# Feed-forward with gate and up products two chunks ahead of the down products, and every inner value turned by DMA

## The reference

```python
def swiglu(x, w_gate, w_up, w_down):
    return (jax.nn.silu(x @ w_gate) * (x @ w_up)) @ w_down

h = h + FFN_RES * swiglu(rms_norm(h, g), w_gate, w_up, w_down)   # T = 256, D = 1024, D_FF = 2816
```

## Time and profile before

| | us |
|---|---|
| median of 3 runs | 1210.16 |
| lowest and highest of them | 1208.95, 1210.77 |
| span of the profiled execution | 1207.7 |
| TensorE busy | 1199.7 |
| VectorE busy | 773.3 |
| ScalarE busy | 691.9 |

### The profile page before, as it was taken

The page is one execution under the profiler, slowest core; times in us unless marked ns, Lnnn a source line. Parts: engine busy times, 40 slices in busy tenths (PEclk is TensorE's granted clock), DMA queues, the critical chain, the costliest instruction groups (busy, mean ns, idle before and its releaser), DMA issues.

```text
span 1207.7 us, 17122 instructions
## 1 busy us (share of the span) xinstructions
PE 1199.7 (99%) x5662; PEld 989.7 (82%) x5662; DVE 773.3 (64%) x1089; ACT 691.9 (57%) x1012; POOL 68.3 (6%) x119
## 2 busy tenths in 40 slices
PE   9999999999999999999999999999999999999998
PEld 7888888877788888888888788888888887888887
DVE  6665555688685556567678766665556667655554
ACT  6555555676655555557666576655555546655543
POOL 0420000000000000000220110000000000000000
PEclk9999999999999999999999999999999999999999
DMA  9977754554465998745654517986655554776771
GB/s 333 245 226 223 216 178 154 167 175 140 157 220 166 244 245 257 217 155 160 201 168 164 174 66 232 252 230 198 200 155 167 164 168 145 213 221 201 219 226 44
DMA packets 208385, 232.01 MB, mean 192 GB/s; under 512 B 56080, under 2 KB 148368, under 8 KB 208336
## 3 DMA queue, kind: packets, MB, share of 16 engines
q1 hardware_dynamic: 163792, 214.61, 57.1%
q10 hardware_dynamic: 42752, 11.02, 5.0%
q0 software_dynamic: 1792, 5.75, 2.0%
HBM read 219.78 MB, written 1.05 MB: 183 GB/s over the span
## 4 chain that ended last, share of the span: by engine, by line
PE 96%; DVE 1%; DMA 1%; ACT 1%; issue 0%; ACTq 0%
PE bank L1971 30%; PE bank L1973 30%; PE bank L1972 30%; PE bank L2030 2%; PE bank L2198 1%; DMA sb_probs<-sb_probs 1%; PE bank L2214 1%; PE bank L2185 1%; PE bank L2183 0%; DMA sb_gates<-h_xT 0%; ACT sb_probs L1237 0%; PE bank L2060 0%; DVE sb_wl L1320 0%; PE bank L2502 0%; DVE sb_rmax L1866 0%
## 5 line engine op out<-in xcount | busy, mean ns | idle before, releaser
L1971 PE MATMUL bank<-sb_wh,sb_aTh 128*128 128x512 f32 (+1 forms) x1124 | 435.6, 388 | 0.0
L1973 PE MATMUL bank<-sb_wh,sb_aTl 128*128 128x512 f32 (+1 forms) x1124 | 431.0, 383 | 0.0
L1972 PE MATMUL bank<-sb_wl,sb_aTh 128*128 128x512 f32 (+1 forms) x1124 | 430.7, 383 | 0.0
L1320 DVE TENSOR_TENSOR sb_wl<-sb_raw,sb_wh 128x1024 fp32r<-128x1024 f32 x269 | 325.4, 1221 | 102.4 <-ACT sb_wh L733 98.1
L733 ACT ACTIVATE sb_wh<-sb_raw 128x1024 fp32r<-128x1024 f32 (+1 forms) x275 | 285.7, 1048 | 117.5 <-PE bank L1973 43.8
L1973 PEld LDWEIGHTS bank<-sb_wh,sb_aTl 128*128 128x128 f32 x1124 | 211.2, 188 | 42.1
L1971 PEld LDWEIGHTS bank<-sb_wh,sb_aTh 128*128 128x128 f32 x1124 | 211.3, 188 | 40.9 <-DVE sb_wl L1320 0.4
L1972 PEld LDWEIGHTS bank<-sb_wl,sb_aTh 128*128 128x128 f32 x1124 | 211.4, 188 | 39.9
L1320 DVE TENSOR_TENSOR sb_wl<-sb_z,sb_wh 128x1024 fp32r<-128x1024 f32 x132 | 158.8, 1222 | 37.0 <-ACT sb_wh L733 36.9
L733 ACT ACTIVATE sb_wh<-sb_z 128x1024 fp32r<-128x1024 f32 x132 | 137.2, 1057 | 58.7 <-PE bank L1973 40.6
L1971 PE MATMUL bank<-sb_wh,sb_hTh 128*128 128x512 f32 x320 | 125.0, 391 | 0.4 <-DVE sb_hTl L1402 0.4
(11 more groups left out here) (218 smaller groups left out, 918.4 us busy)
## 6 DMA issues: line engine op xcount, KB each, us to landing
sb_raw<-w_in SPq DMA_DIRECT2D x80, 256.0 KB, 3.0
sb_z<-ffn_w_down SPq DMA_DIRECT2D x64, 256.0 KB, 4.7
sb_z<-w_down SPq DMA_DIRECT2D x64, 256.0 KB, 3.7
sb_raw<-w_gate SPq DMA_DIRECT2D x54, 256.0 KB, 3.5
sb_raw<-w_up SPq DMA_DIRECT2D x54, 256.0 KB, 4.2
sb_raw<-ffn_w_gate SPq DMA_DIRECT2D x51, 256.0 KB, 3.7
sb_raw<-ffn_w_up SPq DMA_DIRECT2D x51, 256.0 KB, 4.5
sb_raw<-e_w_in SPq DMA_DIRECT2D x40, 256.0 KB, 3.1
```

Of the source, the lines that this page charges most:

```text
L1320: dve.tensor_tensor(wl[:, u % NSPLIT, :], raws[SLOT[u]], wh[:, u % NSPLIT, :].bitcast(F32), ALU.subtract).then_inc(low_done, 1)
L1971: pe.matmul(dst, lh, w_hi, start=start, stop=False)
L1972: pe.matmul(dst, lh, w_lo, start=False, stop=False)
L1973: return pe.matmul(dst, ll, w_hi, start=False, stop=stop)
```

## The change

TensorE's order becomes: gate and up of chunks 0, 1 and 2, down of chunk 0, gate and up of chunk 3, down of chunk 1, ..., gate and up of chunk 10, down of chunks 8, 9 and 10. SP loads the units in that order. Gate and up of chunk 2 go to banks 6 and 7, since banks 0 and 1 still hold chunk 1. The eight transposes per feed-forward on TensorE, `ht_step` and the semaphore `ht_psum` are gone; chunks 0 and 10 take the way of the planes and the DMA as well, so there are 44 DMA transposes and not 36. `hTh` and `hTl` hold one chunk; the parts of chunks 9 and 10 go to `aTh` and `aTl`, whose contents are used up by then. `join_step` now waits until `hT` of the chunk before has been read for its low part. The order of splits and steps on ScalarE and VectorE is written anew:

```diff
 # SP
                 def load_pass(c):
                     for i in range(4):
-                        load_gate_up(u + 4 + i, f, i, c + 1, c)
+                        load_gate_up(u + 8 + i, f, i, c + 2, c)
                     for k in range(2):
-                        load_down(u + 8 + k, f, 2 * c + k, c)
+                        load_down(u + 12 + k, f, 2 * c + k, c)
...
-                for k in range(2):
-                    load_down(u + 64 + k, f, 2 * (NFC - 1) + k)
+                for k in range(4):
+                    load_down(u + 62 + k, f, 2 * (NFC - 2) + k)
 # ScalarE
+                def turned_step(c, dst):
+
+                    act.wait_ge(hT_joined, NFC * f + c + 1)
+                    copy(dst, hT).then_inc(ht_high, 1)
...
-                def body(c, turned, tail_chunk=False, begun=0):
-                    for i in range(begun, 3):
-                        split(u + 4 + i, c)
-                    if turned:
-                        turned_step(c)
-                    split(u + 7, c)
-
-                    act.wait_ge(units_used, u + 8 + 6 * c)
-                    silu_step(c + 1)
-                    split(u + 8, c)
-                    if tail_chunk:
-                        split(u + 9, c)
-                        return
-                    planes_step(c + 1)
-
-                    act.wait_ge(planes_done, (NFC - 2) * f + 1 + c)
-                    split(u + 9, c)
+                def hidden(c, v, c6=0):
+
+                    split(v, c6)
+                    planes_step(c)
+
+                    act.wait_ge(planes_done, NFC * f + c + 1)
+                    split(v + 1, c6)
                     turn_hidden()
+
+                def body(c, bank_=0):
+                    v = u + 8
+                    split(v, c)
+                    split(v + 1, c)
+                    turned_step(c, hTh[:, :, :])
+                    split(v + 2, c)
+                    split(v + 3, c)
+
+                    act.wait_ge(units_used, v + 4 + 6 * c)
+                    silu_step(c + 2, bank_)
+                    hidden(c + 2, v + 4, c)
...
                 silu_step(0, FFN_FIRST_BANK[f])
-                if f > 0:
-                    split(u + 2)
-                split(u + 3)
-                if f == 0:
-                    split(u + 4)
-                ht_step(1, hTh[:, :, :])
+                n = 2 if f > 0 else 3
+                hidden(0, u + n)
                 if f == 2:
                     km_split(1, 4)
                     split(u + 4)
                     km_turn(1)
-                body(0, False, begun=1 if f in (0, 2) else 0)
-                with act.Fori(1, NFC - 2, 1) as c:
-                    body(c, True)
-
-                body(NFC - 2, True, True)
-                ht_step(2, aTh[:, 6:8, :])
+                for i in range(4 if f in (1, 3) else 5, 8):
+                    split(u + i)
+
+                act.wait_ge(units_used, u + 8)
+                silu_step(1)
+                hidden(1, u + 8)
+                split(u + 10)
+                turned_step(0, hTh[:, :, :])
+                split(u + 11)
+
+                act.wait_ge(units_used, u + 12)
+                silu_step(2, 6)
+                hidden(2, u + 12)
+                with act.Fori(1, NFC - 3, 1) as c:
+                    body(c)
+                body(NFC - 3)
+                turned_step(NFC - 2, aTh[:, 4:6, :])
+                splits(u + 62, 2)
+                turned_step(NFC - 1, aTh[:, 6:8, :])
 # VectorE
                 def join_step(c):
 
-                    dve.wait_ge(planes_turned, 16 * (NFC - 2) * f + 16 * c)
+                    if not (isinstance(c, int) and c == 0):
+
+                        dve.wait_ge(ht_low, NFC * f + c)
+                    dve.wait_ge(planes_turned, 16 * NFC * f + 16 + 16 * c)
...
-                def body(c, turned, begun=0):
-                    for i in range(begun, 2):
-                        split(u + 4 + i, c)
-                    if turned:
-                        join_step(c)
-                        turned_step(c)
-                    for i in range(2, 4):
-                        split(u + 4 + i, c)
-                    mul_step(c + 1)
-                    for i in range(2):
-                        split(u + 8 + i, c)
+                def body(c, bank_=0):
+                    v = u + 8
+                    split(v, c)
+                    split(v + 1, c)
+                    turned_step(c, hTl[:, :, :], hTh[:, :, :])
+                    split(v + 2, c)
+                    join_step(c + 1)
+                    split(v + 3, c)
+                    mul_step(c + 2, bank_)
+                    split(v + 4, c)
+                    split(v + 5, c)
...
+                n = 2 if f > 0 else 3
+                splits(u + n, 8 - n)
+                join_step(0)
+                mul_step(1)
+                splits(u + 8, 2)
+                split(u + 10)
+                turned_step(0, hTl[:, :, :], hTh[:, :, :])
+                split(u + 11)
+                join_step(1)
+                mul_step(2, 6)
+                splits(u + 12, 2)
+                with dve.Fori(1, NFC - 3, 1) as c:
+                    body(c)
+                body(NFC - 3)
+                turned_step(NFC - 2, aTl[:, 4:6, :], aTh[:, 4:6, :])
+                split(u + 62)
+                join_step(NFC - 1)
+                split(u + 63)
+                turned_step(NFC - 1, aTl[:, 6:8, :], aTh[:, 6:8, :])
 # TensorE
+                def body(c, bank_=0, start=False):
+                    if bank_ == 0:
+
+                        pe.wait_ge(h_ready, 2 * NFC * f + 4 + 2 * c)
+                    gate_up(u + 8, bank_, c)
+
+                    pe.wait_ge(ht_low, NFC * f + 1 + c)
+                    for k in range(2):
+                        down_unit(u + 12 + k, k, hTh, hTl, c, start and k == 0)
...
-                c = NFC - 2
-
-                pe.wait_ge(h_ready, 2 * NFC * f + 2 + 2 * c)
-                gate_up(c)
-
-                pe.wait_ge(ht_low, NFC * f + 1 + c)
-                down_unit(c, 0)
-                transpose_hidden(c + 1)
-                down_unit(c, 1)
+                body(0, 6, True)
+                with pe.Fori(1, NFC - 3, 1) as c:
+                    body(c)
+                body(NFC - 3)
+
+                pe.wait_ge(ht_low, NFC * f + NFC - 1)
+                for k in range(2):
+                    down_unit(u + 62 + k, k, aTh[:, 4:6, :], aTl[:, 4:6, :])
```

More of the change, by code:

```diff
@@ L301, in two_block_kernel @@
         h_ready = sem("h_ready")
-        ht_psum = sem("ht_psum")
         ht_high = sem("ht_high")
@@ L527, in load_front @@
                     load_gate_up(u, 0, FRONT[u][1], FRONT[u][0])
-                for k in range(2):
-                    load_down(8 + k, 0, k)
             def load_early_unit(u):
```

64 lines of the change are left out of this document (14 added, 50 removed).

## The result

The changed kernel takes 1215.13 us (median of 5 runs, 1212.64 to 1217.00) beside 1210.28 us for the kernel before on the same chip: ratio 1.0039, 95% interval 1.0027 to 1.0052. A second series on another chip gave 1213.34 us (8 runs) beside 1210.50 us: 1.0028, 1.0018 to 1.0039. The change costs 3 to 5 us. The forecast was +1.0 us, 1211.1, range 1207.5 to 1215.5: the range holds the time, but the likeliest case, no measurable change, did not come.

The account below looks back on a forecast made before the run. TensorE's queue of products was taken to bound the kernel; -3.5 (transposes) -0.6 (third feed-forward) +3.4 (ends) +1.7 (front) = +1.0 us on the 1207.7 us span, giving a time of 1211.1 us, range 1207.5 to 1215.5.

Parts of the forecast that it names:

- the likeliest case: Whole kernel: time within 0.2% (2.4 us) of the kernel before, chance 0.60; faster 0.13, slower 0.27.
- Transposes, -3.5 us: TensorE, all feed-forwards: eight groups of four transposes of `hid`, 0.44 us each, disappear, 3.5 us gained.
- Loop, nothing: Inner loop of each feed-forward: ways of 6.0 us + landing, at most 16.5, against 21.8 due; no new wait.
- Ends, +3.4 us: Last chunks of every feed-forward: hTl(9) late behind chunk 10's split and DMA issue, 2 x 0.78 + 2 x 0.9 us.
- Front of the first, +1.7 us: First chunks of first feed-forward: hTl(0) late by 1.6 us, 1.7 with restart, at a landing of 8.6 us.
- landing minus 7.0: First feed-forward's front: loss by landing of the first transpose, nothing at 7.0 us and 3.6 at 10.5.
- the forecast's own sign: First feed-forward's front: step wrong if the first transpose, issued near 24.8 us, lands under 7 us or over 9.
- the rival of slow transposes: First and second feed-forward fronts: first two transposes land in 10.5 us each, +6.9, 1217 us; chance 0.20 with lesser forms.
- its second half: First feed-forward's front: transpose 1, issued at 38.2, lands at 48.7; mul(2) ends at 50.4, late by 2.2 us.
- Third feed-forward, -0.6 us: Front of the third feed-forward: TensorE's wait for hTl of chunk 0 at 770 us goes, 0.64 us gained.
- The 2.5 us: Whole kernel: median of runs, 1210.16, exceeds the profiled span, 1207.7, by 2.5 us and moves with it.
- two rules weighed: Chunk transposes: one skill section prefers TensorE (DMA estimate 10.5 us per chunk); another calls transposing DMAs as fast as ordinary ones.

Follow-up runs that it names:

- the three mends and the padding: Changed kernel with chunk 9's parts ahead of silu of chunk 10, early loads held, memory keys' transpose behind the splits, plus 100 idle TensorE waits: 1207.18 us, 0.9973.
- the three mends alone: Changed kernel with chunk 9's parts ahead of silu of chunk 10, early loads held, memory keys' transpose behind the splits, no idle waits: 1208.70 us, 0.9983.
- the padded kernel: Changed kernel with 100 more waits, on a semaphore already up, in TensorE's program behind the loop of the first feed-forward: 1211.04 us, ratio 1.0003.

## Why the forecast was right and wrong, step by step

- **Transposes, -3.5 us: right.** The second and fourth feed-forward gain 0.20 and 0.19 us, which is -0.88 and the end wait of 0.69.
- **Loop, nothing: right.** No wait for inner values or `h_ready` stands in any of the four loops behind its first pass (the wait at 776 us is at the entry of that pass, where the forecast counts `h_ready` of chunk 2 with the first chunks), with 44 transposes landing in 3.0 to 9.8 us, median 4.2 (36 in 3.1 to 10.5, median 5.3, before).
- **Ends, +3.4 us: right in place, cause and number of waits; 2.8 us in size.** 0.7 us each, not 0.78 and 0.9. Moving the step away removed all four.
- **Front of the first, +1.7 us: right in place; the size is that of the landing.** The forecast took 8.6 us and said "landing minus 7.0". With 8.1 us TensorE was idle for 0.54 us, with 9.8 and 10.2 for 2.3 and 2.5: zero is nearer 7.5. In the profiled execution 7.1 us passed from the landing (34.45) to TensorE's start (41.57), where the forecast had 7.5 (33.35 to 40.85). By the forecast's own sign, a first landing over 9 us, this step failed in the profiled execution and held in that of the second series. The condition of the rival of slow transposes, 8.5 us and more, came in part of the executions for the first transpose; its second half did not, as the second landed after 6.5 us.
- **The clock, missing.** The sum took a stop of TensorE to cost its own length and 0.1 us. Behind the stop of 2.3 us the clock was at its lower level for 3.4 us, which cost 1.6. The earlier trace rows could not warn of it, as TensorE never stood so long there: its longest wait in the list was 1.3 us, at the start.
- **Third feed-forward, -0.6 us: wrong, and the largest miss.** Instead of one wait less there were two waits of 1.0 and 0.7 us. The working asked whether a whole chunk more of time would hide the landing, and it would have. It didn't look at what else is issued on ScalarE's queue between silu and the splits in that one feed-forward. The prediction's own method, every queue that a step is moved past, was not applied to `km_turn(1)`: the forecast left out that this issue, 1.90 us before, now has a DMA transpose 3.4 us ahead of it on the same queue. It took 4.68.
- **The mixer, nothing: missed** by 1.1 to 1.4 us, and not explained. The sum has no term for a stage whose code the change leaves alone.

By the profiled executions: -3.5 + 2.8 (ends) + 2.5 (stop at 39) + 1.6 (clock) + 1.7 (770 and 776) - 0.6 (the old wait, gone with its place) + 1.4 (mixer) = +5.9 of the 6.3 us. A further 0.35 us are one wait at 736 us, where the products of the third feed-forward begin.

That the time fell into the range is in part luck. The upper end had been set for slow transposes, and two of the terms that used it up, the clock and the long issue, were in no rival; the mixer's is not understood even now. The step from span to time was a little off, too. The 2.5 us are the median of three runs less the span of one; in single runs 1.8 us lie around the span of the kernel before (1210.13 less 1208.3) and 2.2 around that of the changed kernel (1216.17 less 1214.0), so 0.4 us of the loss lie outside the span, and no row shows why.

Of the two rules weighed, the Trainium skill's in "VectorE: DVE Perf Modes", section "The three transpose paths", gave an estimate of 10.5 us for a chunk. The trace disagrees: 4.2 us in the median and 3.0 where nothing else moves, and it comes near 10.5 only with weight loads beside it (9.8 us). The Trainium skill's "Advanced Engine Details and Errata", section "X-Bar Transpose (TRN2)", has transposing DMAs as fast as ordinary ones. In landing times the trace agrees, in the median: the weight loads of 256 KB behind the start land after 2.9 to 4.2 us in the median of their groups, and a chunk's transpose, of the same 256 KB (q10 grew from 11.02 to 13.12 MB for eight more), after 4.2 us. Where both are in flight both are slow: the loads issued beside the transpose of 9.8 us took 6.6 to 9.1. In the engines' time the trace doesn't agree: q10's 13.12 MB took 6.0% of it and q1's 214.61 MB 56.8%, which makes a transposed MB 1.7 times as dear as a loaded one.

The version with the three mends and the padding runs in 1207.18 us, 0.9973 (0.9962 to 0.9984) of the kernel before: 3.3 us faster, where the unmended change was 3 to 5 us slower. What of that is the padding the runs can't tell, as the interval overlaps that of the three mends alone.

## What to carry to other kernels

Running further ahead moves the due times in the loop, where there was slack anyway, and costs at the two ends, where the order on the helper engines decides: write out who stands in front of the critical step there, for each instance of the stage and not for one. A step moved from TensorE to a queue must be priced with all that already uses that queue nearby. Before a loss or gain of 2 us in 1210 is put down to a mechanism, find it in the rows of the stage that it should be in: here the median gain of an edit and the place that the profile gave it differed more than once.

## What the runs showed of the hardware that was not expected

- Behind stops of 2.26 and 2.35 us at 39 us TensorE's clock fell to its lower level for 3.4 us; behind stops of 0.5 to 1.6 us it stayed full, and so it did in the padded kernel's profile behind one of 2.46 us. In 43 runs of kernels with that stop the mean clock was below 1.0 in 13; in 59 with the stop filled, shortened or gone, in none.
- A second DMA transpose issued 3.4 to 3.6 us behind another from ScalarE's queue held that queue for 3.4 to 4.95 us; without the one ahead, 1.8 to 2.0 us. Instructions that stand ahead of it on the engine go on (the three splits at 752.92 us).
- The same transpose, issued at 24.6 us, landed after 5.6 us with the weight loads behind it held back and after 9.8 us with them beside it.
- The idle waits in TensorE's program moved the blocks of the instruction queue by 4 us (100 of them) and 8 us (250). 250 in the kernel before changed nothing that can be measured (0.9997, 0.9987 to 1.0006); 100 in the changed kernel went with 2.5 parts in a thousand less, on another chip.
